# Expert values: one gate multiply on VectorE three rows ahead, the rounded copy on ScalarE, the subtract one turn later

## The reference, cut to what matters

```python
def block(args):
    xb, eb, gb = args
    u = u_tab[eb]
    act = jax.nn.gelu(jnp.einsum('td,tkd->tk', xb, u).astype(jnp.float32), approximate=False)
    wts = (gb * act).astype(v_tab.dtype)
    return jnp.einsum('tk,tkd->td', wts, v_tab[eb])
```

## Time and profile before

| | us |
|---|---|
| median of the runs | 1801.78 |
| the two near runs | 1801.33, 1801.78 |
| span of the profiled execution | 1795.7 |
| value stage in it, first matmul to last | 1048.3 to about 1402.8 |

### The profile page before, as it was taken

How to read it: one execution, slowest core, us unless ns; L and a number is a source line. 1 busy time by engine, 2 the same in 40 slices (tenths; PEclk the granted TensorE clock), 3 DMA queues, 4 the chain that set the end, 5 groups by cost and what they waited for, 6 DMA issues and landing times.

```text
span 1795.7 us, 33010 instructions
## 1 busy us (share of the span) xinstructions
PE 1744.2 (97%) x11190; PEld 1547.2 (86%) x11190; DVE 1251.2 (70%) x2359; ACT 942.1 (52%) x1389; POOL 492.9 (27%) x225
## 2 busy tenths in 40 slices
PE   9999989999999999999999999999999999999997
PEld 6799878897878999999999988888888787669996
DVE  4567587876424499067777578888888896667777
ACT  5466577544555544567777643333333575334444
POOL 4246744401568588800000000000000100013332
PEclk9999999999999999999999999999999999999999
DMA  6654443577344478755565687677767783355553
GB/s 216 200 188 141 166 152 118 190 248 266 121 164 150 135 222 228 228 179 172 174 173 173 195 263 239 235 235 236 237 239 236 272 276 122 113 176 187 183 183 113
DMA packets 122839, 347.63 MB, mean 194 GB/s; under 512 B 13904, under 2 KB 46800, under 8 KB 122512
## 3 DMA queue, kind: packets, MB, share of 16 engines
q1 hardware_dynamic: 121248, 339.52, 58.1%
q0 software_dynamic: 1520, 7.21, 1.1%
HBM read 328.84 MB, written 17.83 MB: 193 GB/s over the span
## 4 chain that ended last, share of the span: by engine, by line
PE 84%; DVE 6%; ACT 4%; issue 2%; POOL 2%; DMA 1%; POOLq 0%; DVEq 0%; ACTq 0%
PE banks L934 83%; POOL weight_rest L851 2%; ACT arena L1676 2%; DMA weight_ring<-in_stream 1%; ACT weight_high L1676 1%; PE banks L945 1%; DVE weight_rest L2307 1%; ACT span_exponentials L1676 0%; DVE arena L3110 0%; DVE arena L2991 0%; DVE arena L2348 0%; ACT scratch L1676 0%; ACT L1676 0%; DVE arena L2347 0%; DVE arena L2345 0%
## 5 line engine op out<-in xcount | busy, mean ns | idle before, releaser
L1676 ACT ACTIVATE weight_high<-weight_ring 128x1024 fp32r<-128x1024 f32 x448 | 473.0, 1057 | 453.4 <-PE banks L934 350.4
L851 POOL TENSOR_TENSOR weight_rest<-weight_ring,weight_high 128x1024 fp32r<-128x1024 f32 x165 | 414.4, 2521 | 264.5 <-ACT weight_high L1676 155.0
L2307 DVE TENSOR_TENSOR weight_rest<-weight_ring,weight_high 128x1024 fp32r<-128x1024 f32 x283 | 346.1, 1224 | 156.3 <-ACT weight_high L1676 153.4
L934 PE MATMUL banks<-a_high,weight_high 128*128 128x256 f32 x1216 | 304.0, 288 | 0.2 <-ACT weight_high L1676 0.2
L934 PE MATMUL banks<-a_rest,weight_high 128*128 128x256 f32 x1216 | 297.8, 283 | 0.0
L934 PEld LDWEIGHTS banks<-a_high,weight_high 128*128 128x128 f32 x1216 | 232.6, 191 | 1.5 <-issue 1.1
L934 PEld LDWEIGHTS banks<-a_rest,weight_high 128*128 128x128 f32 x1216 | 232.9, 192 | 0.3 <-issue 0.2
L934 PE MATMUL banks<-weight_high,gated_high 128*128 128x512 f32 x512 | 201.4, 393 | 0.0
L934 PE MATMUL banks<-weight_high,gated_rest 128*128 128x512 f32 x512 | 200.2, 391 | 0.0
L934 PE MATMUL banks<-a_high,weight_rest 128*128 128x256 f32 x1216 | 170.9, 283 | 2.4 <-POOL weight_rest L851 2.4
L934 PE MATMUL banks<-x_high,weight_high 128*128 128x256 f32 x672 | 167.5, 287 | 4.7 <-DVE x_rest L3079 3.7
(11 more groups left out here) (360 smaller groups left out, 3101.5 us busy)
## 6 DMA issues: line engine op xcount, KB each, us to landing
weight_ring<-in_stream SPq DMA_DIRECT2D x512, 512.0 KB, 3.5
arena<-in_stream SPq DMA_DIRECT2D x66, 512.0 KB, 3.3
unit_spill<-small SPq DMA_DIRECT2D x128, 128.0 KB, 3.6
scratch<-unit_spill SPq DMA_DIRECT2D x128, 128.0 KB, 3.2
residual<-in_x SPq DMA_DIRECT2D x2, 512.0 KB, 4.1
arena<-in_mem POOLq DMA_DIRECT2D x2, 512.0 KB, 5.3
arena<-in_ctx POOLq DMA_DIRECT2D x2, 512.0 KB, 4.8
arena<-in_keys POOLq DMA_DIRECT2D x1, 1024.0 KB, 5.2
```

What stands on the lines that cost most here:

```text
L851: nc.gpsimd.tensor_tensor(w_lo[:, e % 2, :], raw(e)[0], w_hi[:, e % 2, :], ALU.subtract).then_inc(S["rest_ready"], 1)
L934: return nc.tensor.matmul(out, lhsT, rhs, start=start, stop=stop, skip_group_check=True)
L1676: return nc.scalar.activation(out, in_, f, **kw)
L2307: tt(w_lo[:, e % 2, :], raw(e)[0], w_hi[:, e % 2, :], ALU.subtract).then_inc(S[ready], 1)
```

## The change

VectorE's `gate_row` keeps only the first multiply, and runs three rows ahead instead of two. ScalarE makes `gated_high` as a copy of `GATED` (`gated_high()`), also three rows ahead, behind the `split_high` of the same turn; it waits for the product and until TensorE has begun the tile that frees the buffer. VectorE makes the rest in a separate `gated_rest()`, for the row two ahead, so one turn after its product. Rows 0 to 2 are made ahead of the loop by VectorE, and by ScalarE behind the units stage. The two signals for the zeroed tile become one, counted 1 and 2.

```diff
+            def gated_high(a, turn=None):
+                i_ = 0 if turn is None else turn
+                act.wait_ge(S["gated_made"], i_ * 4 + (a + 1))
+                if a >= 4:
+                    act.wait_ge(S["hi_begun"], i_ * 4 + (V0 + a - 2))
+                func(gated_hi[:, a % 4, :], GATED[:, a % 4, :], ACT.Copy).then_inc(S["gated_high_ready"], 1)
+
+            for a in range(3):
+                gated_high(a)
+            for a in range(4):
+                split_high(V0 + a + 2)
+                gated_high(a + 3)
+            with act.Fori(0, P // 4 - 2) as i:
+                for a in range(4, 8):
                     split_high(V0 + a + 2, i, 4)
-            for a in range(P - 2, P):
-                split_high(V0 + a)
+                    gated_high(a + 3, i)
+            for a in range(P - 4, P - 2):
+                split_high(V0 + a + 2)
+                if a + 3 < P:
+                    gated_high(a + 3)
...
-                s = a % 4
-                dve.wait_ge(h_in[s], i_ * 16 + 16 * (a // 4 + 1))
-                if a >= 4:
-                    dve.wait_ge(S["hi_begun"], i_ * 4 + (V0 + a - 2))
-                tt(GATED[:, s, :], UNITS_IN[:, s, :], row_, ALU.mult).then_inc(S["gated_made"], 1)
-                tt(gated_hi[:, s, :], UNITS_IN[:, s, :], row_, ALU.mult).then_inc(S["gated_made"], 1)
-                dve.wait_ge(S["gated_made"], i_ * 8 + (2 * a + 2))
-                tt(gated_lo[:, s, :], GATED[:, s, :], gated_hi[:, s, :], ALU.subtract).then_inc(S["p_ready"], 1)
-
-            gate_row(0)
-            gate_row(1)
+                dve.wait_ge(h_in[a % 4], i_ * 16 + 16 * (a // 4 + 1))
+                tt(GATED[:, a % 4, :], UNITS_IN[:, a % 4, :], row_, ALU.mult).then_inc(S["gated_made"], 1)
+
+            def gated_rest(a, turn=None):
+                i_ = 0 if turn is None else turn
+                dve.wait_ge(S["gated_high_ready"], i_ * 4 + (a + 1))
+                tt(gated_lo[:, a % 4, :], GATED[:, a % 4, :], gated_hi[:, a % 4, :],
+                   ALU.subtract).then_inc(S["p_ready"], 1)
+
+            for a in range(3):
+                gate_row(a)
+            for a in range(2):
+                gated_rest(a)
             for a in range(4):
                 split_rest(V0 + a, "lo_ready")
-                gate_row(a + 2)
+                gate_row(a + 3)
+                gated_rest(a + 2)
             with dve.Fori(0, P // 4 - 2) as i:
                 for a in range(4, 8):
                     split_rest(V0 + a, "lo_ready", i, 4)
-                    gate_row(a + 2, i)
+                    gate_row(a + 3, i)
+                    gated_rest(a + 2, i)
             for a in range(P - 4, P):
                 split_rest(V0 + a, "lo_ready")
+                if a + 3 < P:
+                    gate_row(a + 3)
                 if a + 2 < P:
-                    gate_row(a + 2)
+                    gated_rest(a + 2)
```

More of the change, by code:

```diff
@@ L543, in build @@
             g_k g_kd g_H z_made dve_columns ctx_e o_root v_ms v_root rows_used v_ready
-            oc_ready gdiag x3_ready ffn_center ffn_gelu x4_ready out_ready act_step dve_step zeros_ready warm_zeros
+            oc_ready gdiag x3_ready ffn_center ffn_gelu x4_ready out_ready act_step dve_step zeros_ready
             neg_a m_hi_ready m_lo_ready at_hi_ready at_lo_ready y_hi_ready y_lo_ready mg_hi_ready
@@ L548, in build @@
             x1_hi_ready x1_lo_ready x2_hi_ready x2_lo_ready cx_hi_ready cx_lo_ready rest_ready column_ready square_made
-            constants_made slots_negated residual_scaled y_squares y_mean y_root masks_joined log_hi_ready log_lo_ready o_squares epsilon_set gated_made hidden_ready hidden_made summed""".split()
+            constants_made slots_negated residual_scaled y_squares y_mean y_root masks_joined log_hi_ready log_lo_ready o_squares epsilon_set gated_made gated_high_ready hidden_ready hidden_made summed""".split()
         S = {n: sem(n) for n in names}
@@ L958, in keep_busy @@
                     mm(ps[:, 7, :], WARM[:, 0:P], WARM)
-            pe.wait_ge(S["warm_zeros"], 1)
+            pe.wait_ge(S["zeros_ready"], 1)
             keep_busy(5)
@@ L1623, in _ @@
             gates_spread(1)
-            pe.wait_ge(S["zeros_ready"], 1)
+            pe.wait_ge(S["zeros_ready"], 2)
             for t in range(TT):
@@ L1730, in split_high @@
                 func(w_hi[:, e % 2, :], src, ACT.Copy).then_inc(S["hi_ready"], 1)
-            act.wait_ge(S["warm_zeros"], 1)
+            act.wait_ge(S["zeros_ready"], 1)
             func(warmed[:, 15:16], WARM[:, 0:1], ACT.Sqrt)
@@ L2089, in _ @@
                     split_high(U0 + U_EARLY + U_GATED + j + 2, i, 4)
-            with act.Fori(0, P // 4 - 1) as i:
-                for a in range(4):
-                    split_high(V0 + a + 2, i, 4)
-            for a in range(P - 2, P):
-                split_high(V0 + a)
+            def gated_high(a, turn=None):
[11 more added lines that the diff above has]
+                for a in range(4, 8):
+                    split_high(V0 + a + 2, i, 4)
+                    gated_high(a + 3, i)
[3 more added lines that the diff above has]
+                    gated_high(a + 3)
             warm(ACT.Sqrt)
@@ L2307, in split_rest @@
                 tt(w_lo[:, e % 2, :], raw(e)[0], w_hi[:, e % 2, :], ALU.subtract).then_inc(S[ready], 1)
-            signal(V.memset(WARM, 0.0), "warm_zeros")
+            signal(V.memset(WARM, 0.0), "zeros_ready")
             scale_rows(0, D, lambda t: hres[:, t, :], lambda t: XN[:, t, :])
```

## The result

The changed kernel takes 1815.22 us, the kernel before, on the same chip, 1802.3: a ratio of 1.0072 with a 95% interval of 1.0057 to 1.0087, or 12.9 us more. That is slower by less than 2%, as forecast, at 1813.4. Single runs far slower than the rest (3885.57 us once for the kernel before, 2876.13 us once for the run with the row ahead of its tile) are left out of the ratios, each of which is to runs of the kernel before on the same chip.

The account below looks back on a forecast made before the run. TensorE bounds the value stage before; after the change the row-load prefetch distance does. 2.6 + 0.8 + 7 + 1.2 = 11.6 us; 1795.7 + 11.6 + 6.1 = 1813.4 us (+0.6%), range 1803 to 1838.

Parts of the forecast that it names:

- row 0 behind ScalarE's unit work: Value-stage entry: ScalarE's first copy stands behind its last unit output and a weight split, delaying TensorE by 2.6 us.
- half clock behind it: After the entry stall: TensorE's granted clock may drop, costing up to another 1.7 us; taken as 0.
- first loads (row 4, gain row): Start of value stage: row 4's load lands late, +0.8 us (0 to 1.3); gain-row load among the first loads, +1.2 once.
- settled trip: Value stage after the first loads: the unit row's round trip exceeds TensorE's two turns by 0.12 us a pair, +7 us.
- the 61 pairs: Pairs of value-stage turns after the first load, each at 5.66 us where TensorE needs 5.54.
- The bound: Value stage: TensorE is busy all 300 us and waits for nobody, so removing 53.8 us of VectorE work gains 0.
- The trip: Value stage: from one weight rest through row load, multiply and subtract to the rest two on, 5.66 us against 5.54.
- The PE-bound rival: Value stage: TensorE stays the bound after the entry, only entry and first load cost; 1804.4 to 1806.4 us, chance 0.28.
- The slow-landing rival: Value stage: row loads land slowly, median 4.6 us, making the kernel over 2% slower, time 1899; chance 0.14.
- The offset: Whole kernel: median time lies 6.1 us above the profiled span of 1795.7 us, and that difference stays.

Follow-up runs that it names:

- the run with the row ahead of its tile: Changed kernel, but from row 6 on SyncE issues the unit row's load ahead of the same turn's weight tile fetch; 1809.36 us, ratio 1.0030.
- the run with both edits: Changed kernel with unit-row loads issued a turn earlier and rounded copies of rows 0 to 2 made by VectorE ahead of the loop; 1802.88 us, ratio 1.0009.

## Why the prediction was right

Point by point, for the profiled executions:

| term, us | predicted | measured |
|---|---|---|
| row 0 behind ScalarE's unit work | 2.6 | 2.3 of idle time |
| half clock behind it | 0, up to 1.7 | 1.7 |
| first loads (row 4, gain row); measured: loss up to 1100 us | 0.8 + 1.2 | 1.1 |
| settled trip; measured: loss behind 1100 us | 7 | 6.8 |
| longer turn of TensorE | - | about 1 |
| sum | 11.6 | 12.9 |

The idle time is the profile's; the half clock is the first turn's 4.13 and the second's 3.09 us (1057.23 to 1060.32) less twice 2.78. The two lines of loads are the lengths of all turns read from the starts of TensorE's matmuls, counting what is over 2.78 us: 7.9 us in 47 turns, of which 1.1 lie ahead of 1100 us. The prediction cut between the first load and the 61 pairs behind it, so the two lines are best taken together: 9.0 predicted, 7.9 measured. The last term is what remains of the stage's 10.6 us, 0.01 us a turn. The sum is that of two single profiles, and that it meets the ratio's 12.9 us to a tenth is luck, with an interval of 10 to 16. That the forecast's sum came within 1.3 us is luck in part as well: it left out 1.7 us of half clock and about 1 us of longer turns, and had 1.4 us too much in its other terms.

*The bound.* The prediction said that nothing VectorE sheds can come back, since TensorE's pitch fills the stage. The run with both edits bears it out: 125 multiplies less, ratio 1.0009.

*The trip.* Reckoned at 5.66 us for two turns from rows of the kernel before; 5.68 measured, as TensorE's mean pair; single trips scatter about it. The runs moved its parts: one row nearer or one turn earlier removes the loss, one operation more raises it to 45 us, one turn later makes it 359 (the stage is 713.4 us there, 354.8 in before). The landing's length was laid to the 512 KB in front of the row; with the row in front its median stayed 3.2 us, so that reason is not shown. The PE-bound rival was tight against it (2% of the pair) and lost.

*The entry.* Its mechanism was right and the idle time 0.3 us shorter than reckoned. Mis-sized was the clock: I named the 1.7 us and took 0, since one of two rows showed no drop behind a longer idle time. Both rows were in hand and half of the price would have been the better term, the more so since the second profile of the kernel before shows that the very same idle time comes out either way. Windows 62 to 67 us, of the earlier trace rows's execution and of the later one, each behind 2.50 us of idle time:

```profile
62.00:67.00 5.00, 4.96 (x22) 4.12 (x23) 4.42 (x9) 2.12 (x2) 0.00 (x0) 1.00 0.76 218
...
62.00:67.00 5.00, 4.92 (x15) 3.88 (x16) 3.65 (x8) 1.28 (x2) 0.00 (x0) 0.66 0.63 210
```

*The early loads.* 2.0 us were set aside; all the loss up to 1100 us, some seven of the 61 pairs included, was 1.1. The gain row was issued at 1061.94, one load later than I had placed it.

*The slow-landing rival* did not come: from 1070 us on the landings were near the settled ones (median 3.1 up to 1100 us, 3.2 behind it, where three of 106 were above 3.5 and the longest was 4.5).

*The offset.* I carried 6.1 us between span and time through the sum. The profiled execution of the changed kernel took 1812.97 us for a span of 1811.2, so the true offset is 1.8; the remaining 4 us of my 6.1 were then the difference between the execution profiled before and the median. It did no harm as it stood on both sides, but the span of one execution was not good to more than some microseconds, as the second profile of the kernel before shows.

## What to carry to other kernels

Running a consumer further ahead gives it more slack only if its inputs are requested further ahead too: when the request stays tied to the same event, each step of lead is taken from the transfer's time. Add up the trip from the event that issues the load to the next such event, with all that stands behind the load in the waiting engine's order, and compare it with the turns it has. And work handed to an in-order engine starts at the earliest behind what that engine still owes the stage before: look at the first turn of a pipeline by itself.

## What the runs showed of the hardware

A 128 KB load issued 0.37 us *ahead* of a 512 KB one on the same queue did not land sooner in the median (3.2 us) than one issued 0.43 us behind it (3.2, in the kernel before). Its spread was 1.9 to 4.4 us there, against 3.0 to 3.4 us in the kernel before and 2.9 to 4.5 in the changed one, and long and short landings came in stretches.

TensorE was at its lower clock level in the first turns in all five profiles in which it idled 2.26 us at this place, and in none of the six in which it did not, the one with spare matmuls in the gap among them; there the first turn took 2.94 us instead of 4.41. Elsewhere an idle time of 2.50 us kept the upper level in one execution of the kernel before (1.00) and lost it in another (0.66).

A turn of 12 matmuls with 512 columns each, with nothing waited for, took 2.77 us in two profiles of the kernel before and 2.78 or 2.79 in the four kernels in which ScalarE copies in the same stage and nothing is waited for.
